# Dense products that walk their 512 columns from the last to the first

## What is computed

```python
def first_block(x, ...):                    # two layers
    for i in range(DEPTH):
        h = h + 0.5 * swiglu(rms_norm(h), ffn1_gate_up[i], ffn1_down[i])     # 1024 -> 2 x 2816 -> 1024
        q, k, v, ca, cg = split(rms_norm(h) @ w_in[i])
        mixed = concat(norm(sliding_window_attention(q, k, v)), norm(conformer_conv(ca, cg)))
        h = h + mixed @ w_out[i]
        h = h + 0.5 * swiglu(rms_norm(h), ffn2_gate_up[i], ffn2_down[i])
        h = h + sigmoid(h @ w_ple_gate[i]) * rms_norm(p[i] @ w_ple[i])
    return rms_norm(h)

def second_block(x, ...):                   # two layers
    for i in range(DEPTH):
        parts = split(rms_norm(h) @ w_in[i])
        mix = concat(gated_deltanet(...), native_sparse_attention(...), stick_breaking_attention(...))
        h = h + mix @ w_out[i]
        h = h + conv_ffn(rms_norm(h), w_up[i], ffn_conv[i], w_down[i])       # 1024 -> 2 x 2816 -> 1024
        h = h + sigmoid(rms_norm(h) @ w_ple_gate[i]) * rms_norm(p[i] @ w_ple[i])
    return rms_norm(h)
```

## Time and profile before

| | |
|---|---|
| Time, median of 2 runs | 3952.97 us (3952.47 to 3953.47) |
| Profiled execution, span from the first to the last instruction | 3950.6 us |
| TensorE matmuls busy | 3812.4 us, 97% of the span, 17790 instructions |
| TensorE weight loads busy (overlap the matmuls) | 3050.4 us, 77% |
| VectorE busy | 2334.5 us, 59% |
| ScalarE busy | 1510.9 us, 38% |
| GpSimd busy | 511.5 us, 13% |
| Mean DMA rate | 80 GB/s |

### The profile page before, as it was taken

How to read it: one execution, slowest core, us unless ns; L and a number is a source line. 1 busy time by engine, 2 the same in 40 slices (tenths; PEclk the granted TensorE clock), 3 DMA queues, 4 the chain that set the end, 5 groups by cost and what they waited for, 6 DMA issues and landing times. The chain is left out here.

```text
span 3950.6 us, 46607 instructions
## 1 busy us (share of the span) xinstructions
PE 3812.4 (97%) x17790; PEld 3050.4 (77%) x17790; DVE 2334.5 (59%) x3213; ACT 1510.9 (38%) x2188; POOL 511.5 (13%) x366
## 2 busy tenths in 40 slices
PE   8999989999999998999989999999999999999997
PEld 6888758888788885788877678788877767878886
DVE  5455766445544475744467675775567665675656
ACT  3224653223322365322243444343343353343333
POOL 1001731000100055100020013200010002220002
PEclk9999989999999999999999999999999999999999
DMA  4333203333233330233332100122233110022222
GB/s 152 96 96 112 66 21 96 96 96 111 86 98 99 97 106 11 79 100 96 96 114 80 49 22 1 43 96 96 96 109 107 59 38 6 12 80 96 96 96 80
DMA packets 87018, 314.99 MB, mean 80 GB/s; under 512 B 10016, under 2 KB 10400, under 8 KB 86176
## 3 DMA queue, kind: packets, MB, share of 16 engines
q1 hardware_dynamic: 83664, 302.43, 24.4%
q10 hardware_dynamic: 3152, 9.74, 0.7%
HBM read 307.94 MB, written 2.10 MB: 78 GB/s over the span
## 5 line engine op out<-in xcount | busy, mean ns | idle before, releaser
L384 ACT ACTIVATE wh<-raw 128x1024 fp32r<-128x1024 f32 x564 | 597.4, 1059 | 1630.3 <-PE ps L404 1317.5
L402 PE MATMUL ps<-xh,wh 128*128 128x512 f32 x2336 | 918.0, 393 | 16.7 <-DVE xl L467 10.0
L403 PE MATMUL ps<-xl,wh 128*128 128x512 f32 x2336 | 910.8, 390 | 0.0
L404 PE MATMUL ps<-xh,wl 128*128 128x512 f32 x2336 | 910.5, 390 | 0.0
L388 DVE TENSOR_TENSOR wl<-raw,wh 128x1024 fp32r<-128x1024 f32 x564 | 695.6, 1233 | 181.1 <-ACT wh L384 180.2
L402 PEld LDWEIGHTS ps<-xh,wh 128*128 128x128 f32 x2336 | 439.8, 188 | 112.4 <-issue 19.6
L403 PEld LDWEIGHTS ps<-xl,wh 128*128 128x128 f32 x2336 | 440.0, 188 | 94.3 <-issue 3.6
L404 PEld LDWEIGHTS ps<-xh,wl 128*128 128x128 f32 x2336 | 439.8, 188 | 91.9
L402 PE MATMUL ps<-fh,wh 128*128 128x512 f32 x1016 | 397.1, 391 | 4.0 <-DVE wl L388 4.0
L404 PE MATMUL ps<-fh,wl 128*128 128x512 f32 x1016 | 395.4, 389 | 0.0
L403 PE MATMUL ps<-fl,wh 128*128 128x512 f32 x1016 | 395.3, 389 | 0.0
(11 more groups left out here) (467 smaller groups left out, 5529.6 us busy)
## 6 DMA issues: line engine op xcount, KB each, us to landing
raw<-in_w SPq DMA_DIRECT2D x564, 512.0 KB, 3.5
con<-in_consts SPq DMA_DIRECT2D x1, 2053.5 KB, 14.0
h<-in_x SPq DMA_DIRECT2D x4, 512.0 KB, 6.9
p_t<-in_p ACTq DMA_DIRECT2D x4, 512.0 KB, 3.9
w1k<-in_w1c ACTq DMA_DIRECT2D x2, 1024.0 KB, 4.9
w1v<-in_w1c ACTq DMA_DIRECT2D x2, 1024.0 KB, 7.0
out<-h SPq DMA_DIRECT2D x8, 256.0 KB, 2.2
dup_k<-roped ACTq DMA_DIRECT2D x8, 128.0 KB, 3.6
```

Of the source, the lines that this page charges most:

```text
L384: nc.scalar.activation(wh[k % 2][:, :], raw[k % 4][:, :], ACT.Copy).then_inc(s["w_hi"], 1)
L402: nc.tensor.matmul(DB[k % 2][:, :], a, hi(q), start=(q == order[0]), stop=False)
L403: nc.tensor.matmul(DB[k % 2][:, :], a, lo(q), start=False, stop=False)
L404: last = nc.tensor.matmul(DB[k % 2][:, :], b, hi(q), start=False, stop=(q == order[-1]))
```

## The change

In the six matmul calls of `pe_unit` and `pe_chunks`, both the output and the moved operand are given with a step of -1 along the row. Each instruction then reads the 512 columns of the operand from the last to the first, and writes the 512 columns of the bank from the last to the first. The stationary operands, the order of the matmuls, the waits and the increments are as before, and so is every other matmul.

```diff
--- before.py
+++ after.py
@@ -399,9 +399,9 @@  (pe_unit)
                 a, b = wh[k % 2][:, q * P:(q + 1) * P], wl[k % 2][:, q * P:(q + 1) * P]
-                nc.tensor.matmul(DB[k % 2][:, :], a, hi(q), start=(q == order[0]), stop=False)
-                nc.tensor.matmul(DB[k % 2][:, :], a, lo(q), start=False, stop=False)
-                last = nc.tensor.matmul(DB[k % 2][:, :], b, hi(q), start=False, stop=(q == order[-1]))
+                nc.tensor.matmul(DB[k % 2][:, ::-1], a, hi(q)[:, ::-1], start=(q == order[0]), stop=False)
+                nc.tensor.matmul(DB[k % 2][:, ::-1], a, lo(q)[:, ::-1], start=False, stop=False)
+                last = nc.tensor.matmul(DB[k % 2][:, ::-1], b, hi(q)[:, ::-1], start=False, stop=(q == order[-1]))
@@ -409,9 +409,9 @@  (pe_chunks)
                 a, b = wh[k % 2][:, q * P:(q + 1) * P], wl[k % 2][:, q * P:(q + 1) * P]
-                nc.tensor.matmul(DB[k % 2][:, :], a, hi(q), start=start and n == 0, stop=False)
-                nc.tensor.matmul(DB[k % 2][:, :], a, lo(q), start=False, stop=False)
-                last = nc.tensor.matmul(DB[k % 2][:, :], b, hi(q), start=False, stop=stop and n == len(chunks) - 1)
+                nc.tensor.matmul(DB[k % 2][:, ::-1], a, hi(q)[:, ::-1], start=start and n == 0, stop=False)
+                nc.tensor.matmul(DB[k % 2][:, ::-1], a, lo(q)[:, ::-1], start=False, stop=False)
+                last = nc.tensor.matmul(DB[k % 2][:, ::-1], b, hi(q)[:, ::-1], start=False, stop=stop and n == len(chunks) - 1)
```

## The result

The changed kernel takes 4042.68 us (4042.49 to 4042.86) against 3952.97 us, two runs each. The ratio is 1.0222 with a 95% interval of 1.0202 to 1.0242: 89.7 us more, slower by just over 2%. The page of the profile: TensorE has as many instructions as before and is busy 98 us longer, while the busy times of VectorE and ScalarE are those of the earlier trace rows to within a microsecond.

The account below looks back on a forecast made before the run. TensorE's dense matmuls were taken to bound the kernel: time = 3952.97 + 13.06 x d, with d = 0 giving 3953 us. The forecast's own range was 3940 to 3973 us, the wide range 3938 to 6680.

Parts of the forecast that it names:

- The slope of 13.06 us per nanosecond: Kernel time for each nanosecond added to one of the 13056 dense TensorE matmuls.
- d: Extra time per dense matmul from the reversed pattern; taken as 0, between -1 and +1.5 ns.
- the line of 6.0 ns: Extra per dense matmul at which the kernel changes by about 2% (79 us), the least a measurement can tell.
- Rival 2: Fixed price at each dense matmul start, as the walker misses its first line: +12.9 ns, 4121 us; chance 0.07.
- the first rival: Write of all 13056 matmuls: bank takes reversed elements singly, +213.6 ns each, 6499 to 6742 us; chance 0.20.
- The bound of +256: Upper bound in ns on the read side's extra per dense matmul, from a neighbouring row whose floor hides anything below 2.2 times.
- the bound of +213.6: Upper bound in ns on the write side's extra per dense matmul, if the bank took one element instead of two.
- pairs that stay pairs: Argument for a free backward bank write: the same neighbours stay together, 511 with 510, 509 with 508; value 0.
- Rival 3: Operand read: each column fetches its line anew, up to +256 ns, 7295 us; chance 0.08 with anything between.
- Rival 4: Faster: the gap between two dense matmuls closes, -12.9 ns each, -168 us, 3785 us; chance 0.02.
- the seam: The 12.9 ns between two dense matmuls, left of 226.2 ns beyond the 213.3 ns that 512 columns need.
- 78 us off a rival: Deduction from the first rival's 2789 us: at most 2.8% of time runs at clock 0.50, already paying 427 ns.

Follow-up runs that it names:

- The small kernel: Separate kernel computing nothing of the reference: 48 dense matmuls back to back per form, 21 forms; 226.7 ns forward, 233.3 ns turned on both sides.

## Why the prediction was right or wrong

**What bounds the kernel: right.** One product's slot times 13056 is what moved. The slope of 13.06 us per nanosecond held after two small terms that the sum had not: 7.6 us absorbed by waits, 12 us added by the clock.

**The forecast, d = 0, was wrong**, and the measured d is 6.6 ns. It lies above the line of 6.0 ns that the text drew, and outside the forecast's own -1 to +1.5 ns; the likeliest outcome, no change (0.63), became 2.2% slower. The wide range held the time by luck: it reached through the second rival to the first, and neither of their mechanisms occurred.

**The step that failed is the value taken for the read side**, "so on the read side I take 0"; measured, it is 6.6 ns. The bound of +256 held, but it bounded nothing useful. The value had two supports. The first was line 2013, in which a read with a step of 8 floats shows no price. By the text's own words a floor hides there anything below 2.2 times, and the price is 1.03 times. The step from there to the dense product also passed over the format: line 2013 is plain fp32, whose columns go at 0.84 ns in each of a product's two matmuls, and the dense products are in the reduced format at 0.44. The small kernel shows what that hides. In plain fp32 a backward read is free (429.2 and 429.2); in the reduced format it costs 6.6 ns, and a step of 2 takes 229.9 instead of 120.0 ns. The second support, that the backward walk touches the same neighbours, holds only inside a group of four floats (226.7): when the groups themselves come in falling order, 233 ns is paid. Why it is paid is open.

**The write side: right in its value**, and the bound of +213.6 stood for something that didn't occur: "pairs that stay pairs" was argued, and the write-only run shows the freedom but not that reason. The rule of the Trainium skill (Advanced Engine Details and Errata, section PSUM Cachelines), read by its letter, had been made the first rival with a chance of 0.20; it came out false for this pattern.

**Rival 2 had the shape and not the mechanism.** It priced a fixed loss at each start at 12.9 ns and 4121 us; the loss is half that and isn't fixed, since it is absent at 336 columns and below. **Rival 3 had the place** (the read), with a size of 256 ns at most that was 39 times too large; the text gave it together with everything between 0.08. The true case, a small price on the read, lay between these two rivals, and neither was priced for it. **Rival 4**: no run closed the seam.

**What the text said would show it** did: 859 matmuls from 100 to 300 us lie between the 884 of the forecast and the 836 of rival 2, and name d before any sum is made. At 1.2 GHz the spacing is 427 ns before and after, the time of 512 columns, so neither the seam nor the price shows there; the 0.42 to 0.43 us of the earlier trace rows let one expect as much.

**Not foreseen:** the 12 us in untouched matmuls. The prediction used the mean clock only to take 78 us off a rival, as if the clock were a constant of the kernel.

## What to carry to other kernels

A bound from a neighbouring row holds only at the same rate: before a row of another format or width is laid on the hot loop, compare their nanoseconds per column, for the slower one can hide what the faster one pays, and see whether the row rests on a floor, for then it says little. Where a stream of matmuls is the bound, turn the write and not the read, or turn the read in blocks of 128: both are free here, while a backward read of 512 columns in the reduced format costs 3% of the product. And when one nanosecond is 13 us, "nearly contiguous" needs a measurement.

## What the runs showed of the hardware

- The reduced fp32 format has a seam of 226.7 - 213.3 = 13.3 ns between 512-column matmuls at 2.4 GHz, the same 13.3 at 256, 320 and 384 columns, 16.0 at 448 and 16.7 at 480, and none at 1.2 GHz (427). Bfloat16 has 2.5 ns (215.8). A record of plain fp32 takes 429.2 ns, 2.5 more than twice 213.3. The Trainium skill, TensorE: Matmul & The Clock Gate, section "Wait — 56ns, not 53.3ns?", gives 215.7 ns for a warm matmul (at 2.4 GHz) of 512 columns, to which the bfloat16 row agrees; the reduced fp32 rows are 11 ns above it.
- A step of 2 on the moved operand halves the speed in the reduced format (229.9 against 119.9 ns for 256 columns).
- Sixteen floats turned inside blocks that go forwards are the dearest order found, 266.6 ns, against 233.3 for a full turn.
- With weights of 32 columns (load 108 ns instead of 188) a forward matmul of the reduced format is slower, 231.8 instead of 226.7 ns. Whether by the shorter load or by the fewer output rows isn't shown, and what joins all these numbers is open.
- Repeated runs of one kernel differ by the clock: the runs of before at 0.986 took 3952 to 3953 us, those at 0.984 and 0.985 3953 to 3961, and one each at 0.982 and 0.980 took 3964 and 3968.
